# Seven heads' outputs turned by transposing DMAs of their 16-bit halves, in a two-layer mLSTM and pooling kernel

## The reference, cut to what matters

```
proj = x @ w_in                       # three projections: xm, z, o_pre (2048 columns each), and gates
q, k = from silu(conv(xm)), v = from xm, per head (8 heads of 256 columns)
h    = chunkwise mLSTM(q, k, v, gates)                # (1024, 8, 256)
hn   = (h - mean(h)) * rsqrt(var(h) + eps) * norm_g   # per head, over its 256 columns
hb   = sigmoid(o_pre) * hn + skip * silu(conv(xm))
x    = LayerNorm(alpha * x + (hb * silu(z)) @ w_out)
```

## Time and profile before

| | |
|---|---|
| median of 3 runs | 1388.76 us (1388.63 to 1389.24) |
| the profiled execution | 1388.8 us, of it 1387.0 us of span |
| TensorE busy | 1373.3 us, 99% |
| VectorE busy | 1156.7 us, 83% |
| ScalarE busy | 753.4 us, 54% |
| GpSimd busy | 147.7 us, 11% |
| granted TensorE clock | 0.998 of full speed |
| moved by DMA | 213.44 MB |

### The profile page before, as it was taken

How to read it: one execution, slowest core, us unless ns; L and a number is a source line. 1 busy time by engine, 2 the same in 40 slices (tenths; PEclk the granted TensorE clock), 3 DMA queues, 4 the chain that set the end, 5 groups by cost and what they waited for, 6 DMA issues and landing times.

```text
span 1387.0 us, 19098 instructions
## 1 busy us (share of the span) xinstructions
PE 1373.3 (99%) x6602; PEld 1150.4 (83%) x6602; DVE 1156.7 (83%) x1891; ACT 753.4 (54%) x1318; POOL 147.7 (11%) x246
## 2 busy tenths in 40 slices
PE   9999999999999999999999999999999999999997
PEld 7788888888888888888888888888888888888886
DVE  7989989898989989899874446797888888899976
ACT  5875765748576675757733436564333333346340
POOL 1002011010201111010000001001111111110021
PEclk9999999999999999999999999999999999999999
DMA  6115344362433426245497667434656555699661
GB/s 231 53 39 145 93 118 118 77 174 62 137 100 98 139 67 175 70 138 177 138 337 241 221 192 226 126 118 115 168 159 162 158 140 149 174 294 342 214 198 76
DMA packets 103809, 213.44 MB, mean 154 GB/s; under 512 B 11010, under 2 KB 27906, under 8 KB 102562
## 3 DMA queue, kind: packets, MB, share of 16 engines
q1 hardware_dynamic: 90914, 178.66, 38.7%
q0 software_dynamic: 12800, 33.56, 13.0%
HBM read 170.11 MB, written 75.63 MB: 177 GB/s over the span
## 4 chain that ended last, share of the span: by engine, by line
PE 94%; DVE 3%; DMA 1%; ACT 1%; issue 1%; POOL 0%; DVEq 0%; SPq 0%; ACTq 0%; POOLq 0%
PE wide L2935 20%; PE wide L2937 20%; PE wide L2936 20%; PE ps_state L2935 3%; PE ps_state L2937 3%; PE ps_state L2936 3%; PE ps_inter L2936 2%; PE ps_inter L2935 2%; PE ps_inter L2937 2%; PE ps_intra L3114 2%; PE ps_intra L2937 2%; PE ps_intra L2935 2%; PE ps_s L2935 2%; PE ps_s L2937 2%; PE ps_s L2936 2%; PE ps_intra L2936 2%
## 5 line engine op out<-in xcount | busy, mean ns | idle before, releaser
L2936 PE MATMUL wide<-xa,inb 128*128 128x512 f32 x576 | 224.7, 390 | 0.0
L2935 PE MATMUL wide<-xb,inb 128*128 128x512 f32 x472 | 189.4, 401 | 0.8 <-DVE z_buf L1978 0.8
L2937 PE MATMUL wide<-xb,inb 128*128 128x512 f32 x472 | 184.3, 391 | 0.0
L2936 PEld LDWEIGHTS wide<-xa,inb 128*128 128x128 f32 x576 | 108.4, 188 | 20.3
L2936 PE MATMUL wide<-xa,blk 128*128 128x512 f32 x320 | 124.5, 389 | 0.0
L2937 PEld LDWEIGHTS wide<-xb,inb 128*128 128x128 f32 x472 | 88.6, 188 | 19.1
L2935 PEld LDWEIGHTS wide<-xb,inb 128*128 128x128 f32 x472 | 88.8, 188 | 18.1 <-issue 1.2
L2935 PE MATMUL wide<-xb,blk 128*128 128x512 f32 x256 | 99.6, 389 | 0.0
L2937 PE MATMUL wide<-xb,blk 128*128 128x512 f32 x256 | 99.6, 389 | 0.0
L1860 ACT ACTIVATE wy<-wy_raw 128x1024 fp32r<-128x1024 f32 x56 | 59.3, 1061 | 63.3 <-DMA wy_raw<-y_block 63.2
L2935 PE MATMUL wide<-xa,inb 128*128 128x512 f32 x208 | 83.4, 401 | 3.0 <-ACT z_buf L1221 2.0
(11 more groups left out here) (439 smaller groups left out, 3950.2 us busy)
## 6 DMA issues: line engine op xcount, KB each, us to landing
in_raw<-in_w_in SPq DMA_DIRECT2D x45, 512.0 KB, 4.2
wy_raw<-y_block SPq DMA_DIRECT2D x56, 256.0 KB, 4.7
mw_raw<-h_block SPq DMA_DIRECT2D x53, 256.0 KB, 3.4
m_sum<-in_w_out POOLq DMA_DIRECT2D x48, 256.0 KB, 4.2
h_block<-f_buf SPq DMA_DIRECT2D x48, 256.0 KB, 3.2
w_sum<-in_pool_w_out POOLq DMA_DIRECT2D x48, 256.0 KB, 4.3
a_raw<-in_pool_w_z SPq DMA_DIRECT2D x16, 512.0 KB, 3.9
a_raw<-folded SPq DMA_DIRECT2D x16, 512.0 KB, 4.6
```

The lines of the kernel that those rows point to most:

```text
L2935: pe.matmul(dst, a[0], b[0], start=first, stop=False, skip_group_check=more)
L2936: pe.matmul(dst, a[0], b[1], start=False, stop=False, skip_group_check=more)
L2937: return pe.matmul(dst, a[1], b[0], start=False, stop=last, skip_group_check=more)
```

## The change

For heads 0 to 6 TensorE no longer turns the output. ScalarE takes each half of `num` apart into its lower and upper 16 bits (`part_turn`, two instructions a half), SyncE moves each part with one transposing DMA (`move_turned`, two a half, of 128 x 1024 elements of 16 bits), and ScalarE joins the parts to float32 in SBUF (`join_turn`, two a half). VectorE's `y_turned` reads that in place of PSUM. The transposed parts go to the place of `num`, the parts taken apart and the joined result to the place of `qT` and `kT`. The second pair of DMAs waits until the first has landed. The order on ScalarE, VectorE and SyncE changes: `norm_head` of the second half goes ahead of `first_tap`, `scales` of the second half comes earlier on VectorE, `high_qkv` moves behind the joins, and the four `y_turned` and three `y_finish` come in `second_half`. Two semaphores of the later stages are dropped and their counts continue on the two new ones.

```diff
+            with ExitStack() as whole:
+                turned_halves = sA("turned_halves", [P, 2 * NC * (DV + 1)], U16, whole)
             num = sA("num", [P, NC, DV + 1])
...
+            with ExitStack() as whole:
+                apart = sA("apart", [P, 2, 2, S], U16, whole)
+            with ExitStack() as whole:
+                joined = sA("joined", [P, 2, 2, HALF], F32, whole)
             qT = sA("qT", [P, S])
...
+        def turned_at(f, part):
+
+            at = f * (2 * S + PAD) + part * S
+            return turned_halves[:, at:at + S].rearrange("p (n t) -> p n t", t=P)
...
-        x0_hi = sem("x0_hi")
+        x0_hi, X0_HI = h_apart, 2 * (HEADS - 1)
...
-        wg_in = sem("wg_in")
+        wg_in, WG_IN = h_moved, 64 * (HEADS - 1)
...
+            def move_turned(h, f):
+
+                sp.wait_ge(h_apart, 2 * h + f + 1)
+                if f:
+                    sp.wait_ge(h_moved, 64 * h + 32)
+                for part in range(2):
+                    sp.dma_start_transpose(turned_at(f, part), apart[:, f, part, :]).then_inc(h_moved, 16)
...
                 load_in(3 * h + 1, 1)
+                move_turned(h - 1, 0)
                 load_qkv(h)
                 load_in(3 * h + 2, 0)
                 load_rows(h)
-                store_h(h - 1, 1, 2)
+                move_turned(h - 1, 1)
                 load_in(3 * h + 2, 1)
-                store_h(h - 1, 5, 3, 7)
+                store_h(h - 1, 1, 2, 5, 3, 7)
...
             def high_xm(h, n):
                 act.wait_ge(conv_ready, 2 * h + 2)
-                if h == 0:
+                if h:
+                    act.wait_ge(turn_taken, 4 * h)
+                else:
...
+            def part_turn(h, f, part):
+
+                act.wait_ge(hn_ready, 2 * h + f + 1)
+                act.wait_ge(s_full, NC * (h + 1))
+                ins = act.activation(apart[:, f, part, :].rearrange("p (c d) -> p c d", d=DV),
+                                     num[:, 4 * f:4 * f + 4, 0:DV].bitcast(U16).rearrange("p c (d b) -> p c d b", b=2)[:, :, :, part], ACT.Copy)
+                if part:
+                    ins.then_inc(h_apart, 1)
+
+            def join_turn(h, f, part):
+
+                act.wait_ge(h_moved, 64 * h + 32 * (f + 1))
+                ins = act.activation(joined[:, f, :, :].bitcast(U16).rearrange("p j (c t b) -> p c j t b", t=P, b=2)[:, :, :, :, part],
+                                     turned_at(f, part).rearrange("p (c j) t -> p c j t", j=2), ACT.Copy)
+                if part:
+                    ins.then_inc(turn_full, 2)
...
                 take_num(h - 1, 6)
+                part_turn(h - 1, 0, 0)
+                part_turn(h - 1, 0, 1)
                 take_num(h - 1, 7)
                 in_high(x + 10)
                 in_high(x + 11)
+                in_snapshot(3 * h + 1, 1)
                 in_high(x + 12)
-                in_snapshot(3 * h + 1, 1)
+                norm_head(h - 1, 1)
+                part_turn(h - 1, 1, 0)
+                part_turn(h - 1, 1, 1)
                 first_tap(h, 1)
                 in_high(x + 13)
-                high_qkv(h)
-                norm_head(h - 1, 1)
                 in_high(x + 14)
...
                 in_snapshot(3 * h + 1, 6)
+                join_turn(h - 1, 0, 0)
+                join_turn(h - 1, 0, 1)
                 in_upper_right(3 * h)
+                join_turn(h - 1, 1, 0)
+                join_turn(h - 1, 1, 1)
                 in_snapshot(3 * h + 1, 5)
                 in_high(x + 16)
                 in_high(x + 17)
+                high_qkv(h)
...
                 in_sum(3 * h + 1, 0)
-                y_turned(h - 1, 0)
+                chunk_stats(h - 1, 6)
                 in_sum(3 * h + 1, 1)
-                y_turned(h - 1, 1)
+                chunk_stats(h - 1, 7)
+                scales(h - 1, 1)
                 in_low(x + 10)
-                chunk_stats(h - 1, 6)
                 in_sum(3 * h + 1, 2)
+                norm_scale(h - 1, 1)
                 in_sum(3 * h + 1, 3)
                 in_join(3 * h, 4)
-                chunk_stats(h - 1, 7)
-                scales(h - 1, 1)
                 in_low(x + 11)
                 in_join(3 * h + 1, 2)
-                y_finish(h - 1, 0)
-                norm_scale(h - 1, 1)
+                in_low(x + 12)
                 tap(h, 1, 1)
-                in_low(x + 12)
-                y_finish(h - 1, 1)
                 in_low(x + 13)
                 in_low(x + 14)
                 in_low(x + 15)
-                y_turned(h - 1, 2)
-                y_finish(h - 1, 2)
...
                 tap(h, 1, 2)
                 tap(h, 1, 3)
+                y_turned(h - 1, 0)
+                y_turned(h - 1, 1)
                 in_sum(3 * h + 2, 0)
+                y_finish(h - 1, 0)
+                in_join(3 * h + 1, 5)
+                y_finish(h - 1, 1)
+                y_turned(h - 1, 2)
+                y_finish(h - 1, 2)
                 y_turned(h - 1, 3)
-                in_join(3 * h + 1, 5)
                 in_low(x + 16)
                 in_low(x + 17)
...
-                if h:
-                    if (kind, q) == (X_OF, 5):
-                        turn_head(h - 1, 0)
-                    elif (kind, q) == (Z_OF, 1):
-                        turn_head(h - 1, 1)
-                    elif (kind, q) == (Z_OF, 6):
-                        turn_head(h - 1, 2)
-                    elif (kind, q) == (Z_OF, 7):
-                        turn_head(h - 1, 3)
```

More of the change, by code:

```diff
@@ L32 @@
 F32R = mybir.dt.float32r
+U16 = mybir.dt.uint16
 P = 128
@@ L578, in build @@
         hn_ready = sem("hn_ready")
+        h_apart = sem("h_apart")
+        h_moved = sem("h_moved")
         turn_full = sem("turn_full")
@@ L1363, in group_hi @@
                 else:
-                    act.wait_ge(wg_in, 16 * (g + 1))
+                    act.wait_ge(wg_in, WG_IN + 16 * (g + 1))
                 raw, hi, _ = group_part(g, m)
@@ L2112, in y_turned @@
                 at = COL_G + 2 * h + j
-                turned = (ps_inter, ps_s)[m % 2][:, :] if b is None else b
+                turned = joined[:, n, j, :] if b is None else b
                 dve.wait_ge(turn_full, 4 * h + m + 1)
@@ L2553, in first_half_lo @@
             def first_half_lo(n):
-                dve.wait_ge(x0_hi, n + 1)
+                dve.wait_ge(x0_hi, X0_HI + n + 1)
                 at = (B11, B21)[n // 4]
@@ L3131, in turn @@
                 mm.then_inc(turn_full, 1)
-            def turn_head(h, m):
-                if m == 1:
-                    pe.wait_ge(s_taken, NC * (h + 1))
-                elif m:
-                    pe.wait_ge(turn_taken, 4 * h + m - 1)
-                turn(h, m, (ps_inter, ps_s)[m % 2])
             pe.wait_ge(const_set, 2)
```

## The result

The changed kernel takes 1414.6 us, median of four executions (1413.3 to 1416.9), against 1389.0 (1388.6 to 1389.6) for the kernel before: 1.0178 times as long, interval 1.0163 to 1.0194. It was to be 1399, and by the prediction's own range for this mechanism 1407 at most. The direction was right, the size was not: 25.6 us more in place of 10.

A forecast was written before the change was run, and what follows sets the result against it. The prediction held the head loop bound by TensorE, VectorE close behind with 7 us to spare in 81.6. 1388.8 - 12.6 (turns) + 7 x 3.3 (O6 late) = 1399.3, said as 1399; range 1394 to 1407, overall 1378 to 1425.

The forecast's parts named there:

- what the turns take of TensorE: Each turn of four transposes costs TensorE 0.45 us: 1.8 a head, 12.6 saved over 28 turns if nothing takes it back.
- idle ahead of the tap: VectorE's tap(h,1,1) waits for ScalarE's first_tap and starts at 290.3 instead of 288.27, opening 3.4 us of idle.
- where TensorE would wait and for whom: TensorE waits about 0.9 us ahead of Z4 and 2.4 ahead of O6, seven times, on VectorE's join and in_low.
- the DMAs are hidden: Transposing DMAs take 5 to 7 us a pair, land in time for ScalarE's joins and add nothing beyond VectorE's walk.
- the last term of the sum: O6 (O projection, product 6) starts 3.3 us a head after its new deadline, Z4's 0.9 included, in seven heads.
- Behind O6 nothing more is late: After O6 low_qkv comes at 317.6, values want it at 318.1; each head pays once, 7 x 1.5 = 10.5 us.
- The walk: VectorE's operations in order from the late tap at 290.3: join of Z5 done 299.35, O6 at 309.9; chance 0.48.
- The ceiling: Full gain if the 12.6 us of turns leaving TensorE's queue all leave the time: 1376.2 us, with VectorE keeping pace.
- VectorE's walk has slack: Part of the faster rival: VectorE's order holds slack counted as work, so the turns' gain stays; shared chance 0.24.
- The late pair: Second pair of transposing DMAs lands late, holding VectorE; each us over 7 costs 7, a 10 us pair gives 1420; 0.2.
- ScalarE quick enough: ScalarE's 16-bit copies take half of 1.0 us, so first_tap ends earlier and the kernel gets faster, to 1376.2; 0.24.
- No change: Whole kernel: the turns' gain and the late VectorE cancel, 1386 to 1391.5 us; chance 0.08.

The follow-up runs named there:

- the dummies: Changed kernel with dummy transposes filling TensorE's waits ahead of Z4 and O6: 12 and 20 in one version, 9 and 15 in another; 1412.1 and 1412.7 us.
- The first experiment: Changed kernel with ScalarE's first_tap and the in_high behind it moved back ahead of norm_head and the second pair of part copies; 1415.2 us, 1.0176.
- The reordered version: Changed kernel, same operations: first_tap ahead of norm_head, second joins later, VectorE's taps and y operations spread, in_low of O6 earlier; 1396.2 us, 1.0042.
- the run with the short mask: Changed kernel with GpSimd's mask covering one of eight chunks for heads 1 to 7, same place in its order; 1414.4 us, 1.0166.

## Why the prediction was right in direction and wrong in size

**Held.** The bound (TensorE, VectorE close behind), what the turns take of TensorE (1.83 us a head, 1.8 forecast), 3.45 us of idle ahead of the tap (3.4 forecast), where TensorE would wait and for whom, and that the DMAs are hidden (shown by the run without them).

**Failed: the last term of the sum, "7 x 3.3 (O6 late against its new deadline, Z4's 0.9 included)".** It was 5.6 in place of 3.3. The span grew by 26.7, and with the 12.6 of the turns that is 39.3 over seven heads. The term failed in two ways.

*The clock, 1.2 of the 2.3.* "Behind O6 nothing more is late [...] so each head pays once" is the sentence that fell. In five heads of seven the clock fell to 1.2 GHz for 3.4 us right behind the wait, 1.7 us each, 8.5 in all. The run's granted clock says the same: 0.992 of 1413.7 leaves 11.3 us, 0.998 of 1387.0 (with the clock of the table) 2.8, and the difference is 8.5, within the rounding of the clock. The sum had no term for it, and no rival either. That a fall costs the period 1.7 us is shown by the distances of O6 in the version without copies; in the changed kernel they differ by 1.4. What removing the falls gives is less clear: four falls less came with 7.3 us less of span where the operand of O6 was made earlier, but with the dummies all five went, and only 2 to 3 us came back.

*The walk, 1.1 of the 2.3.* Against its new deadline (308.41 - 1.83 = 306.58) O6 was 4.4 late in place of 3.3: Z4 1.74 in place of 0.9, and 2.65 more up to O6 in place of 2.4. O6 came at 310.97, not 309.9. Of this 0.7 had arisen when the join of Z5 was done (forecast 299.35, measured 308.45 - 8.44 = 300.0): the pair of `in_low` beside the mask took 2.18, where the prediction counted 1.2. It could have been read ahead of time, for the kernel before has the same pair:

```profile
291.40 2.18 DVE L1941 TENSOR_TENSOR inb<-in_raw,inb 128x512 fp32r<-128x512 f32 x2
```

Where that is mended, the load of O's half is the next in line (0.84). The other 0.4 lies between the join and O6, 10.9 us where the prediction counted 10.5; of it 0.25 are the four y operations, which took 2.65 (308.37 to 311.02) and not 2.4.

**The cause was put too far ahead.** The prediction held the 3.4 us of idle in front of the tap to be what makes O6 late. The first experiment took this idle away and the time stayed. What decides is how late the join of Z5 comes, and the work behind it. The join releases TensorE's next three products, 8.16 us; VectorE now has 10.9 us of work from that join to the operand of O6, 2.66 more than before. Per head: -1.83 (turns) + 2.65 (O6 behind Z4: 10.81 in place of 8.16) + 1.74 (Z4 late) = +2.6, and a period without a fall is indeed longer by 2.6 (the values start 84.17 apart, before 81.55). Without the copies Z4 is only some 0.1 late: -1.83 + 2.65 + 0.1 = +0.9, and its periods are 82.6, +1.05. These two runs settle the split; the copies' share is Z4's wait, and the fall in one more head. The reordered version shows it from the other side: its join starts 4.5 us ahead of Z4, so that the 13.04 us behind it make O6 only 1.1 late (9.24 behind Z4 in place of 8.16), and 18 us come back. Moving the operand of O6 alone is not enough, since the waits then come up elsewhere in full, 25.5 us in both.

**The ceiling was taken too high.** 12.6 us leave TensorE's queue, but with the turns free of charge only 6 leave the time. The rival that VectorE's walk has slack was wrong: the reordered version brings 18 of the 26 us back, and what is left waits for VectorE again, at O6 and at the values.

**Rivals.** The late pair: excluded for the changed kernel, seen in the version with the mask moved. ScalarE quick enough: the parts took 1.05, the joins 1.36. No change: no.

**Open.** Why the clock fell in five heads and not in the other two, with the same 1.92 us of wait ahead; why the dummies gave back so little; and which transfers made the pairs late in the version with the mask moved.

## What to carry to other kernels

Before work is taken off the bound engine at a price elsewhere, run the kernel with that work simply left out: here it showed that at most 6 us were to be had in the old order, so the price elsewhere had to stay under that. Where an engine close to the bound hands over operands, count its work between the operation that releases the bound engine and the next operand that this one wants, and keep moved work out of that stretch, or have the releasing operation early by as much; idle time further ahead may not matter at all. And a wait of 2 us on TensorE should carry a term for the clock behind it: in this kernel nothing or 1.7 us each time, which did not simply add to the other waits.

## What the runs showed of the hardware

- The granted clock fell to 0.50 behind waits of 1.9 us on a TensorE that had been busy without a gap for over 5 us, and stayed there for 3.4 us, in five of seven heads. In the run with the operand of O6 earlier it fell once, behind a wait of 1.95 ahead of Z4, and not behind one of 2.77. With dummy transposes in the waits it fell in none of the seven, though up to 1.6 us of wait were left ahead of Z4.
- A transposing DMA of 128 x 1024 elements of 16 bits landed in 3.1 to 6.6 us, median 4.7, and took 1.23 to 3.75 us of SyncE's queue, median 1.35. The Trainium skill (VectorE: DVE Perf Modes, The three transpose paths) gives 1309 ns for a block of 128 x 128; eight times that would be an estimate of 10.5, which the rows do not bear out, so it is no rate.
- A ScalarE copy of 1024 16-bit elements took 1.05 us with a strided read and 1.36 with a strided write.
- GpSimd's mask reads and writes SBUF. Its row in the changed kernel's timeline of GpSimd:

```profile
300.21 1.40 POOL L1129 TENSOR_SCALAR_AFFINE_SELECT m_bc<-m_bc 128x1024 f32<-128x1024 f32 x1 [8.41 <-DMA qw<-wi_rows]
```

  It ended at 301.61 and stretched the pair of `in_low` beside it that began at 300.58 from 1.3 to 2.18 us; in the run with the short mask the pair took 1.38. The Trainium skill (SBUF — State Buffer, Who interferes with whom) states this: a VectorE instruction with two inputs in SBUF contends with a GpSimd instruction that reads SBUF. The rows agree.
